# Gates applied on the way out of PSUM, and gathers that add into nine row buffers, in a two-layer hybrid decoder step

## The reference, cut to what matters

```python
gate = g_p * top_p / jnp.sum(top_p, -1, keepdims=True)
...
yb = lax.map(expert_block, (xb, blk_e)).reshape(cap, shp[-1])
y = jax.ops.segment_sum(yb * buf_w[:, None], buf_t, num_segments=n_tok + 1)[:n_tok]
...
def _layer_out(h, mix, w_out, ln1_g, ln1_b, ...):
    x = _layer_norm(ALPHA * h + mix @ w_out, ln1_g, ln1_b)
    return _layer_norm(ALPHA * x + _hier_moe(x, ...), ln2_g, ln2_b)
```

## Time and profile before

| | us |
|---|---|
| median of 3 executions | 3744.78 (3742.56 to 3762.97) |
| the profiled execution, its own time | 3757.84 |
| its span from first to last instruction | 3755.1 |
| PE busy in the span | 3255.4 (87%) |
| DVE busy | 1275.1 (34%) |
| ACT busy | 913.3 (24%) |
| POOL busy | 584.7 (16%) |

### The profile page before, as it was taken

The page is one execution under the profiler, slowest core; times in us unless marked ns, Lnnn a source line. Parts: engine busy times, 40 slices in busy tenths (PEclk is TensorE's granted clock), DMA queues, the critical chain, the costliest instruction groups (busy, mean ns, idle before and its releaser), DMA issues.

```text
span 3755.1 us, 54741 instructions
## 1 busy us (share of the span) xinstructions
PE 3255.4 (87%) x22252; PEld 2009.0 (54%) x22252; DVE 1275.1 (34%) x3192; ACT 913.3 (24%) x1913; POOL 584.7 (16%) x587
## 2 busy tenths in 40 slices
PE   5998789998898978999499978999989999698990
PEld 2446667776666543333244566777767655334330
DVE  3112444444443351111341134444444334410116
ACT  0001233443443201111110113334434321011111
POOL 0000011111100004344300001111110000233333
PEclk9996798999989988999799859899999899799995
DMA  8112122222213219995631211222221132599826
GB/s 244 56 38 67 43 76 76 71 74 76 73 54 115 76 57 384 402 416 217 239 122 43 83 37 62 76 76 76 70 74 35 67 118 83 204 389 413 350 79 224
DMA packets 168613, 519.40 MB, mean 138 GB/s; under 512 B 41456, under 2 KB 82352, under 8 KB 143024
## 3 DMA queue, kind: packets, MB, share of 16 engines
q0 software_dynamic: 65600, 337.74, 23.5%
q1 hardware_dynamic: 83184, 106.86, 9.5%
q10 hardware_dynamic: 19584, 71.31, 4.8%
HBM read 630.21 MB, written 86.89 MB: 191 GB/s over the span
## 4 chain that ended last, share of the span: by engine, by line
PE 75%; DVE 9%; DMA 6%; ACT 4%; issue 2%; DVEq 2%; SPq 1%; POOL 0%; ACTq 0%; POOLq 0%
PE ps L762 66%; PE ps L759 10%; DMA w_slots<-in_w_gu,rowA 3%; DVE grams L2117 2%; DMA c_x<-xd 1%; DVE S_all L2517 1%; SPq L441 1%; ACT PT L1854 1%; DVE PT L2540 1%; ACT S_all L1823 0%; ACT kT L1583 0%; DMA c_b<-ybd,dga 0%; DVE c_x L2155 0%; ACT PT L1583 0%; DMA xb<-xd,idall 0%
## 5 line engine op out<-in xcount | busy, mean ns | idle before, releaser
L762 PE MATMUL ps<-w_slots,xbT 128*64 128x512 f32 (+1 forms) x2048 | 468.9, 610 | 30.9 <-DMA w_slots<-in_w_gu,rowA 27.5
L762 PE MATMUL ps<-hT,w_in 128*128 128x512 f32 x896 | 392.3, 599 | 3.8 <-ACT hT L1583 3.2
L762 PEld LDWEIGHTS ps<-w_slots,xbT 128*64 128x64 f32 x2048 | 168.0, 140 | 287.6 <-issue 279.8
L762 PE MATMUL ps<-grams 128*128 128x128 f32 (+1 forms) x2448 | 295.2, 276 | 28.7 <-DVE grams L2117 22.4
L762 PEld LDWEIGHTS ps<-grams 128*128 128x128 f32 (+1 forms) x2448 | 273.5, 189 | 49.8 <-issue 28.0
L762 PEld LDWEIGHTS ps<-hT,w_in 128*128 128x128 f32 x896 | 171.4, 192 | 217.9 <-issue 211.7
L762 PE MATMUL ps<-w_out,o_mixT 128*128 128x512 f32 x576 | 260.5, 599 | 1.3 <-DVE o_h L2738 1.3
L1583 ACT ACTIVATE kT<-ps 128x512 f32<-128x512 f32 x320 | 188.1, 596 | 253.8 <-PE ps L759 251.7
L762 PE MATMUL ps<-w_slots,hidT 128*64 128x512 f32 (+1 forms) x1024 | 234.0, 598 | 2.0 <-ACT hidT L1583 1.2
L2907 DVE SCALAR_TENSOR_TENSOR gt<-gt,ps 128x256 f32<-128x256 f32 x64 | 26.9, 421 | 521.6 <-ACT gt L2062 521.6
L759 PE MATMUL ps<-cst,S_all 128*128 128x128 f32 x832 | 158.9, 309 | 19.7 <-ACT PT L1583 19.7
(11 more groups left out here) (376 smaller groups left out, 5158.2 us busy)
## 6 DMA issues: line engine op xcount, KB each, us to landing
ybd<-yb ACTq DMA_DIRECT2D x64, 512.0 KB, 8.2
pd<-stage SPq DMA_DIRECT2D x56, 256.0 KB, 2.3
out_y<-c_h ACTq DMA_DIRECT2D x27, 512.0 KB, 2.9
w_in<-in_w_in SPq DMA_DIRECT2D x6, 2048.0 KB, 32.0
o_mixT<-mixd SPq DMA_DIRECT2D x18, 512.0 KB, 3.5
o_h<-out_y SPq DMA_DIRECT2D x18, 512.0 KB, 4.8
xd<-o_x ACTq DMA_DIRECT2D x18, 512.0 KB, 2.9
c_x<-xd ACTq DMA_DIRECT2D x18, 512.0 KB, 6.8
```

The lines of the kernel that those rows point to most:

```text
L762: return pe.matmul(out, lhsT, rhs, start=start, stop=stop, skip_group_check=True)
```

## The change

The gate moves from the rows gathered to the rows as they leave PSUM. `route` now also builds a table `gslot` (one gate for each row of each pair) with the same one-hot products on PE that it uses for the row ids: 18 more products, one selecting product, and on DVE one 128x576 multiply ahead of the copy of `r_part`, with two copies behind. The two evictions of `yb` multiply by a column of `gslot` instead of copying. Gates carry a factor 1/ALPHA, so the residual row is taken as it is, and the scaling by ACT is gone. The gathers add into `c_x` in the transfer itself (`compute_op=ALU.add`): `add_first` waits for the tile's rows, `add_second` for the first add. `c_x` has nine buffers; `c_a` and `c_b` are gone, and with them four instructions per tile on ACT and DVE (one and two) and the waits for their reuse. Four tiles are loaded up front and the store of tile t is followed by the load of tile t+4. `load_w_in` no longer waits for gathers. The zero stores move from the start to behind the fourth tile of latent rows of layer 0, from another source buffer, and `vec`, `shp`, `cvs`, `rows` of layer 0 are loaded ahead of `w_in`. Buffers `r_gown`, `r_gpart`, `r_tok` and a gap that keeps `r_col` out of the weight slots are added.

```diff
-            def gather(l, t):
-
-                if t >= 3:
-                    pool.wait_ge(dve_m.sem, dve_m.at(("norm", l, t - 3), "v"))
-                for k, c in enumerate((c_a, c_b)):
-                    pool.indirect_dma_start(c[t % 3][:], None, ybd[:], bass.IndirectOffsetOnAxis(ap=dga[:, TILES * k + t:TILES * k + t + 1], axis=0)).then_inc(ya_in[t % 3], 16)
+            def add_first(l, t):
+
+                pool.wait_ge(x_in[t], 16 * (l + 1))
+                pool.indirect_dma_start(c_x[t][:], None, ybd[:], bass.IndirectOffsetOnAxis(ap=dga[:, t:t + 1], axis=0),
+                                        compute_op=ALU.add).then_inc(ya_in[t], 16)
+
+            def add_second(l, t):
+                pool.wait_ge(ya_in[t], 16 * l)
...
                 pool.wait_ge(yb_out, 16 * NPAIR * (l + 1))
+                for t in four:
+                    add_first(l + 1, t)
                 for t in three:
-                    gather(l + 1, t)
+                    add_second(l + 1, t)
                 for t in range(TILES):
                     ln_root(("norm", l + 1, t))
+                    if t + 4 < TILES:
+                        add_first(l + 1, t + 4)
                     if t + 3 < TILES:
-                        gather(l + 1, t + 3)
+                        add_second(l + 1, t + 3)
...
             def store_rows(l, t):
                 act.wait_ge(dve_m.sem, dve_m.at(("norm", l, t), "x"))
                 act.dma_start(y_dram[t * P:t * P + P], c_h[t % 3][:]).then_inc(y_out[t % 3], 16)
-                if t + 3 < TILES:
-                    load_x(l, t + 3)
+                if t + 4 < TILES:
+                    load_x(l, t + 4)
...
             def load_w_in(l):
 
-                if l:
-                    sp.wait_ge(ya_in[2], 32 * (3 * (l - 1) + 1))
...
                 if l == 0:
                     load_norm(0)
-                    sp.wait_ge(dve_m.sem, dve_m.at("init", "zero"))
-                    sp.dma_start(mixd[NPT], c_h[2][:]).then_inc(zero_out, 16)
-                    sp.dma_start(pd.rearrange("(f p) t -> p f t", p=P)[:, :, 0:LEAD], c_h[2][:, 0:NF * LEAD].rearrange("p (f t) -> p f t", f=NF)).then_inc(zero_out, 16)
+                    load_state(0)
                     load_w_in(0)
                     load_layer(0)
-                    sp.wait_ge(zero_out, 32)
                 for f in range(NF):
                     store_feature(l, 0, f)
                 for t in four:
                     store_rows_in(l, t)
+                if l == 0:
+                    sp.wait_ge(dve_m.sem, dve_m.at("init", "zero"))
+                    for q in range(2):
+                        sp.dma_start(mixd[NPT][:, 512 * q:512 * q + 512], stage[4][:]).then_inc(zero_out, 16)
+                    sp.dma_start(pd.rearrange("(f p) t -> p f t", p=P)[:, :, 0:LEAD], stage[4][:, 0:NF * LEAD].rearrange("p (f t) -> p f t", f=NF)).then_inc(zero_out, 16)
...
                 else:
-                    dve.wait_ge(ya_in[u], 32 * (3 * (l - 1) + t // 3 + 1))
-                    dve.wait_ge(act_m.sem, act_m.at(("norm", l, t), "ax"))
-                    for k, c in enumerate((c_a, c_b)):
-                        dve.scalar_tensor_tensor(c_x[u][:], c[u][:], gates[:, k, t:t + 1], c_x[u][:], ALU.mult, ALU.add)
-                        dve.drain()
-                variance(("norm", l, t), c_x[u])
+                    dve.wait_ge(yb_in[t], 16 * l)
+                    variance(("norm", l, t), c_x[t], 1e-5 / ALPHA ** 2)
...
-                tt(gates[:, 0, :], s2, cst[:, C_VALID:C_VALID + TILES], ALU.mult)
+                dve.scalar_tensor_tensor(gates[:, 0, :], s2, 1 / ALPHA, cst[:, C_VALID:C_VALID + TILES], ALU.mult, ALU.mult)
                 dve.drain()
                 tt(gates[:, 1, :], gates[:, 0, :], s4, ALU.mult)
+                dve.drain()
+                tt(r_gown, r_own[:], bc(gates[:].rearrange("p k t -> p (k t)"), [P, 2 * TILES, NPAIR]), ALU.mult).then_inc(dve_m.sem, dve_m.mark(k_, "goh"))
                 dve.wait_ge(pe_m.sem, pe_m.at(k_, "part"))
...
-                    dve.tensor_copy(yb[:, 0:512], pD[:, 0:512]).then_inc(dve_m.sem, dve_m.mark(k, f"yb{p}"))
+                    dve.tensor_scalar(yb[:, 0:512], pD[:, 0:512], gslot[:, p:p + 1], None, ALU.mult).then_inc(dve_m.sem, dve_m.mark(k, f"yb{p}"))
```

More of the change, by code:

```diff
@@ L253, in plan @@
         T["pe"].plan(("lg", l, NPT), ["xT", "lg"])
-        T["pe"].plan(("route", l), ["rank", "be", "part", "ids"])
+        T["pe"].plan(("route", l), ["rank", "be", "part", "ids", "gpart"])
         T["act"].plan(("route", l), ["e1", "e2"])
-        T["dve"].plan(("route", l), ["E7", "E8", "diag", "rows", "oh0", "oh1", "part", "ids"])
-        T["pe"].plan(("moe", l), ["xT0", "gu0", "xT1"])
+        T["dve"].plan(("route", l), ["E7", "E8", "diag", "rows", "oh0", "oh1", "goh", "part", "ids", "gpart", "gslot"])
+        T["pe"].plan(("moe", l), ["xT0"])
+        T["pe"].plan(("route", l), ["gsel"])
+        T["pe"].plan(("moe", l), ["gu0", "xT1"])
         T["act"].plan(("moe", l), ["xT0", "gu0", "xT1"])
@@ L281, in build @@
         consts_in, zero_out = sem("consts_in"), sem("zero_out")
-        x_in, y_out, ya_in = ([sem(f"{n}{u}") for u in three] for n in ("x_in", "y_out", "ya_in"))
+        y_out = [sem(f"y_out{u}") for u in three]
+        x_in, ya_in, yb_in = ([sem(f"{n}{t}") for t in range(TILES)] for n in ("x_in", "ya_in", "yb_in"))
         lnr_in, state_in, w_mix_in, window_in = (sem(n) for n in ("lnr_in", "state_in", "w_mix_in", "window_in"))
@@ L313, in build @@
         with ExitStack() as s:
-            c_a, c_b, c_x, c_h = ([sb(f"c_{n}{u}", [P, D], scope=s) for u in three] for n in "abxh")
+            c_x, c_h = ([sb(f"c_{n}{u}", [P, D], scope=s) for u in range(k)] for n, k in (("x", TILES), ("h", 3)))
             lnr = sb("lnr", [P, 2 * D], scope=s)
@@ L418, in load_layer, with load_state @@
                     sp.wait_ge(dve_b.sem, dve_b.at(("att", l - 1, NPT - 1), "a"))
+                if l:
+                    load_state(l)
+                for dst, src in ((flat(wuqn), "wuqn"), (flat(wuqr), "wuqr"), (wuk[:], "wuk"), (wuv[:], "wuv"),
+                                 (wlora[:], "wlora"), (wgate[:], "wgate")):
+                    sp.dma_start(dst, a[src][l]).then_inc(w_mix_in, 16)
+            def load_state(l):
                 for dst, src in ((vec[:], "vec"), (shp[:].rearrange("p f t -> p (f t)"), "shp"), (cvs[:], "cvs")):
@@ L1507, in last_slot @@
                 mm(Q[3][:, 0:NPAIR], r_part[:], cst[:, C_SEL4:C_SEL4 + 32], True, True).then_inc(pe_m.sem, pe_m.mark(("route", l), "ids"))
+                pe.wait_ge(dve_m.sem, dve_m.at(("route", l), "goh"))
+                for c in range(2 * TILES):
+                    g = 32 * (c % 4)
+                    m = mm(Q[2][g:g + 32, P:2 * P], r_gown[:, c, :], r_col[:, c, :], c < 4, c >= 2 * TILES - 4)
+                m.then_inc(pe_m.sem, pe_m.mark(("route", l), "gpart"))
             def experts(l):
@@ L1589, in load_x @@
                     act.wait_ge(x_out, 16 * TILES * l)
-                act.dma_start(c_x[t % 3][:], src[t * P:t * P + P]).then_inc(x_in[t % 3], 16)
-            def scaled(l, t):
-                act.wait_ge(x_in[t % 3], 16 * (l * 3 + t // 3 + 1))
-                act.activation(c_x[t % 3][:], c_x[t % 3][:], ACT.Copy, scale=ALPHA).then_inc(act_m.sem, act_m.mark(("norm", l, t), "ax"))
+                act.dma_start(c_x[t][:], src[t * P:t * P + P]).then_inc(x_in[t], 16)
             def store_rows(l, t):
@@ L2092, in experts @@
                 store(NPAIR - 1)
-                for t in three:
+                for t in four:
                     load_x(l + 1, t)
-            for t in three:
+            for t in four:
                 load_x(0, t)
@@ L2105, in _ @@
                 experts(l)
-            for t in three:
-                scaled(L, t)
             for t in range(TILES):
                 store_rows(L, t)
-                if t + 3 < TILES:
-                    scaled(L, t + 3)
         @block.vector
```

56 lines of the change are left out of this document (27 added, 29 removed).

## The result

The changed kernel takes **3787.08 us** (median of 4 runs, 3782.04 to 3787.77) against 3746.12 us for the kernel before in the same comparison (4 runs, 3742.56 to 3762.97): ratio 1.0097, 95% interval [1.0075, 1.0118]. That is +41 us, slower, inside the range, and more than twice the forecast of +18.8. The profiled execution took 3787.77 us (span 3786.0), at the median; that of before was 12 us above its own.

What follows compares the result with a forecast made beforehand. PE bounds three quarters of the span, so only start, middle seam and last seam pay. Start -14.0, routing +1.4, middle seam +13.3 and last seam +18.1 sum to +18.8 on 3744.8: 3764 us, range 3750 to 3790.

Steps and rivals of the forecast that it cites:

- Start, -14.0: Kernel start: without the 8-byte pieces tile 4 lands sooner, first product at 33.4 instead of 46.8 us; -14.0 in all.
- that is this stretch: Start, 13 to 27 us at 65 GB/s: identified with the zero store into `pd` of 1792 pieces of 8 bytes.
- 8.6 MB at 400 GB/s: Start: data preceding the end of the first `w_in` slice, said to take 23 us and be in time.
- Zero stores at nothing: Moved zero stores fall where transfers are nearly idle: no cost; 14 us without the cover of the stage buffers.
- Routing, +1.4: Routing of both layers: a 128x576 multiply ahead of the `r_part` copy delays ids some 0.7 us, twice; +1.4.
- First row of a seam, +4.1 and +3.5: First row in middle and last seam: two chained adds, priced at 8.6 and 8.3 us each, delay it +4.1 and +3.5.
- The round, 6.3 + L: Seams: each row waits for the load (L) the previous row released; 6.3 + L a tile, 11.15 us at L = 4.85.
- Tail, 18.2: End of last seam, 3755.0 to 3773.2: tile 8's second add, then last statistics, two rows and the store.
- the forecast's 31.4: Both seams: predicted loss of +13.3 us in the middle seam and +18.1 us in the last.
- first rival of the forecast: Adds are dearer: 3 us more each in moving or POOL's issue, +26, giving 3790 us; chance 0.20.
- the 5.3 + 1.3 of the forecast: Last seam, first add of tile 8: lightest gather's 5.3 us plus 1.3 us for reading what it adds to.
- third rival: Faster: loads under 1 us land before POOL reaches them, DVE's 4.45 us a tile sets the pace; 3704 us; chance 0.06.

Runs made afterwards that it cites:

- s1: Kernel before with only the change's start (zero stores and state loads placed as there), its three buffers and plain gathers kept: 3741.57 us, ratio 0.9977.
- s2: Changed kernel with gathers landing in own buffers, three of each kind, and DVE doing both adds: 3728.37 us, ratio 0.9935.
- r4: Changed kernel with plain gathers overwriting `c_x` instead of adding, same waits and order, sum left out: 3731.6 us, ratio 0.9957.
- r2: Changed kernel with all nine tiles loaded at once in both seams, POOL's order unchanged: 3736.93 us, ratio 0.9972.
- s3: Changed kernel with first gather adding onto `c_x` (six buffers), second landing in its own buffer and added by DVE: 3718.91 us, ratio 0.9912.
- r3: Changed kernel with all nine loads at once, next tile's root ahead of later adds, first adds six tiles ahead: 3756.98 us, ratio 1.0015.

## Why the prediction was wrong in size

The direction, the mechanism and its place were right; the sizes of the seams were not. The step that failed is the price of an adding transfer, taken from plain gathers: 8.6 and 8.3 us to land ahead of the first rows, 0.95 us of POOL's time in each round. By the forecast's own steps:

- **Start, -14.0: right** (the first product 15.6 us sooner, where 13.4 were forecast). Tile 4 had landed when DVE came to it, so x3 ended at 28.1 and not at 30.3. s1 shows that it is the place of the stores and not the buffers. But "that is this stretch" was too simple: the tiny packets had gone by 17 us, and the slow stretch outlasted them to 27. A slip without effect: 8.6 MB at 400 GB/s take 21.5 us, not 23.
- **Zero stores at nothing: right.** The packets near 150 us stand in a window in which PE is busy 50.00 of 50 us.
- **Routing, +1.4: slightly high.** From the start of the page table to the last id DVE takes 10.2 us where it took 9.7, so +1.0 for two layers. That is what the forecast's own rows give, 0.78 less the wait of 0.26; its 0.7 was the slip. An eviction of `yb` costs 0.69 and 0.75 us instead of 0.60 and 0.69, and in s2, which has it too, nothing of it shows.
- **First row of a seam, +4.1 and +3.5: this step failed.** It was +11.8 (36.5 us after the store, not 24.7) and +7.0 (31.8, not 24.8). Each add was priced at the gathers under load, 8.6 and 8.3 us, 17.2 and 16.6 for the two. The two adds of tile 0 took 22.8 us in the middle (1813.58 to 1836.41, when DVE starts on them) and 19.0 in the last seam (3678.39 to 3697.37). Tile 1's second add landed 3.3 and 2.4 us later, and row 0 waits for it, which the forecast had not seen: it counted tile 1's statistics as work of 1.8 us, with its rows at hand. So the last add came 26.2 and 21.4 us after the first issue, +9.0 and +4.8 against the price; 1.8 us were counted too much, and 0.5 us too little for the landing of the load. In r4, with plain gathers in the same order, the first rows end 27.3 and 25.6 us after the store, where the forecast had 28.8 and 28.3: the path was right, and the price of the adding was not.
- **The round, 6.3 + L: right in form.** It is the 12.5 us piece of chain above. The five rounds of the last seam took 62.9 us, 12.58 each, not 11.15. L averaged 5.12 (4.29 to 5.52) against 4.85, so the load was priced well. The term that was off is POOL's: the two issues take 3.4 us and not 2.5, +0.9 a round, with 0.27 for the wait that ends at the load. r4's rounds in the last seam took 10.4 us. In the middle three rounds took 43.2 and not 38.1: +5.1, 2.8 by POOL's issues, 0.8 by the waits' ends and 1.6 by the loads, which were 7.53, 7.84 and 5.40 where 7.9, 6.4 and 4.85 were taken.
- **Tail, 18.2: right** (18.8).

The differences of these steps are 7.7 and 5.1 us in the middle, 3.5, 7.2 and 0.6 in the last seam, less 2.2 up to the last store of layer 0: within 0.1 of the 21.8 us between +18.8 and +40.6.

Most of it has one cause, that an adding transfer beside others is not a gather with one more read of 1.3 us. r4 takes out the adding alone and gets 34.8 us back; the 20.6 us of loss that it leaves in the seams lie below the forecast's 31.4. This is the first rival of the forecast, "adds are dearer", in moving and in POOL's issue: it gave 3790 us, and 3787 was measured. It put 12 us on the first rows (11.2 found), 8 on the rounds (12.3) and 6 on the end (0.6), so that its sum came this near is in part luck. At the end, with little beside it, the first add of tile 8 landed in 6.59 us, the 5.3 + 1.3 of the forecast. I held 0.20 for it and should have held more. The profile of before held no adding transfer, so the nearest row was chosen over the one sentence that spoke of such transfers. The rule of the Trainium skill ("Collectives: The Full Stack", section "The bandwidth ceiling: the fold count and why AG ≠ RS ≠ AR"), which stands there for collectives, is that an add in a transfer halves its throughput. The trace agrees: 180 against 332 GB/s for the same rows and bytes, 1.85 times the time of the engines.

The third rival (rows at DVE's pace) fell with the change as it is: DVE was busy 22.64 of 76 us. Its condition, a load under 1 us, was wrong by the forecast's own sum: the round is 6.3 us with no load at all, above the 4.45 of DVE. Only loads that are not issued behind the row can meet it, as in r2; even then adds set most of the pace in the last seam, 6.3 to 8.4 us a row from x2 to x6, beside 4.3 where DVE alone set it.

A correction to what stands ahead of the prediction: three instructions per tile are gone (one on ACT, two on DVE), not four. No sum uses it.

What stays open: by which part of the transfer the adding costs its time (the second read, or waits between pieces), why POOL takes 0.6 us more to issue it, and how a store of tiny pieces holds back packets that come after its own. No run separates these.

## What to carry to other kernels

Moving an add from an engine into a gather moves it onto the transfer queue, where here it cost nearly as much as a second gather, and onto the path to the first row if the row is waited for. In this kernel it paid to add one operand in flight, where other work covered it, and the other on the engine (s3); two chained adds lost to that even with all loads up front (r2). When buffers are multiplied, move the loads with them: a load issued behind a row's store, whose landing an in-order engine waits for ahead of the next row's work, turns the buffers into a serial round. When a forecast rests on the price of something that the trace does not hold, as the adding here, give the dearer rival the weight that the missing row deserves. Ahead of the first rows of a kernel, look for stores with pieces of a few bytes and put them behind the work that fills PE.

## What the runs showed of the hardware

- An indirect gather of 128 rows of 4 KB took 0.94 to 0.98 us to issue on POOL when plain (r4) and 1.53 to 1.58 us when it added into SBUF (the change), in both with DVE idle in the rounds. Issued right behind a root while DVE worked, plain ones took 1.6 to 2.0 us too (before, last seam).
- The 9.44 MB of a seam took 52.4 us of all 16 engines as adding gathers (180 GB/s) and 28.4 us as plain ones (332 GB/s). The second adds of tile 1, for which the first row waits, took 9.7 and 12.9 us to land in the changed kernel; with all nine loads up front second adds of the first tile took 15.0 and 17.6 (r2), and one of tile 2 took 21.7 with more adds in flight (r3). A first add with little beside it took 6.6 (the change, tile 8).
- With a store of 1792 pieces of 8 bytes in flight, all transfers, those of ACT's loads too, moved 65 GB/s from 13 to 27 us. The tiny packets passed by 17 us; from 17 to 27 none was left and the rate was 63 GB/s. The same stretch without the zero stores ran at 389 to 391 (the change, s1). At its later place the store landed 13.5 us after its issue.
